# Two decoder blocks with product-key experts on one core: the search for experts spread over the blocks of weights, and three blocks multiplied in f32

## The chip, the cores and the metric

The kernel runs on 1 core of one Trainium2 chip, as one program. The metric is the device time of one execution in microseconds (us); the median of the runs counts.

## The reference, cut to what matters

256 tokens of width 1024 go through two decoder blocks. The first has four mixers (attention with forget gates, gated delta rule, two gated linear attentions) and a convolved gated FFN. The second has two attentions and, as its FFN, product-key retrieval over 16384 experts. All is f32. The part around the change is this FFN:

```python
q = (xc @ w_query).reshape(PEER_TOKEN_CHUNK, PEER_HEADS, 2, PEER_HALF)
s1 = jnp.einsum('thd,hnd->thn', q[:, :, 0], sub_keys_1)
s2 = jnp.einsum('thd,hnd->thn', q[:, :, 1], sub_keys_2)
v1, i1 = lax.top_k(s1, 16)
v2, i2 = lax.top_k(s2, 16)
cand = v1[..., :, None] + v2[..., None, :]
cand_idx = i1[..., :, None] * 128 + i2[..., None, :]
best, pos = lax.top_k(cand, 16)
idx = jnp.take_along_axis(cand_idx, pos, axis=-1)
g = jax.nn.softmax(best, axis=-1)
act = jax.nn.gelu(jnp.einsum('td,thkd->thk', xc, expert_u[idx]), approximate=False)
return jnp.einsum('thk,thkd->td', g * act, expert_v[idx])
```

(xc is the normed token, 8 heads, 16 experts a head.)

## The kernel before, in words

**Dense experts.** The kernel gathers experts only for 32 tokens (NG). For the other 224 (NT) it multiplies every expert: `expert_u` is walked in 64 blocks of 256 experts ("block q", the first pass), then `expert_v` in 64 blocks (the second pass). A block is 1 MB, a tile of 128 x 2048 f32. It is loaded by SP's queue into one of three slots of a ring of five (slots 0 to 2; a fourth, slot 3, joins in the second pass). Since TensorE (PE) multiplies f16 faster than f32, a block is split into two f16 halves that are scaled by 64: ACT writes the high half (`expert_hi`, line 2886), DVE the low half (`expert_lo`, line 2139), and PE makes three f16 products for one f32 product (`three`, lines 678, 681 and 684). So a block of the first pass is 2 x 8 x 3 = 48 matmuls of 128 x 224 (`expert_in`). The tokens are kept as f16 halves `xh`, `xl` as well.

**Buffers of halves.** There are seven. Numbers 0 to 3 take blocks 0 to 3; after that numbers 4, 5 and 6 rotate. They lie over `HT` (4, the f32 tokens), `X` (5) and ring slot 4 (6, in which the sub-keys land). `expert_hi(n)` waits until PE has finished block n-3. Six blocks (EARLY) are split before the search begins, while PE still makes the queries; the tables EARLY_HI and EARLY_LO say after which query group.

**The barrier.** After the queries all engines meet in `phase(1)` (DVE's side is line 1392). Then PE multiplies queries by sub-keys (line 1274, 32 f32 products), ACT copies them out of PSUM (line 2450), and DVE starts the search.

**The search on DVE.** `chosen` is a chain of 37 pieces: 12 of choosing for tokens 0 to 127 (`choose(0)`, lines 2154 to 2180), 6 of naming (`name_slots(0)`, lines 2192 to 2243), 8 of `choose(1)`, `slots_evicted(0)`, 4 more of `choose(1)`, 6 of `name_slots(1)`. The last piece of a naming waits for ACT's exponentials (line 2953, `gate_exp`). DVE runs 8 pieces first, and then one list per block q: `slots_evicted(1)` in the list behind the second SLOTS_AFTER; `one_hots` (lines 2275, 2278, 2280) for block q+1 if that has gates; `expert_lo(q+2)`; SEARCH[q] pieces of `chosen` (two for q = 0, 1, 2, then one); `weigh` of block q-1's gates (line 2289); `weigh_late(q-1)` (line 2303); and the gathered rows. An engine works its list strictly in order.

**ACT's list for block q:** `gelu(q)` (lines 2912, 2915; it waits for PE's block q), the exponentials if q is in EXP_AFTER, `expert_hi(q+3)`, `gated_hi` for block q+2 (line 2924), `keep_gates` of block q (line 2934).

**Gates.** `slots(t)` turns the named slots over on PE behind the blocks of SLOTS_AFTER (13 and 26); it waits for `slots_named`. From block LATE = 28 to block 61, 28 groups of 8 tokens are expanded to dense gates: one group is 16 matmuls of 128 columns (line 1314), woven into the block from its 13th matmul on. GATES_IN leaves out blocks 33, 38, 44, 49, 55 and 60. PE waits inside the block for `one_hots`.

**Loads.** SP's queue issues the loads in order. A load waits until its slot's last content has been read, which the list `read` in `sync_program` says: for a block of experts it is `expert_lo` of the block three before.

**Gathered rows.** For the 32 tokens POOL gathers 32 rows of `expert_u` and 32 of `expert_v` per partition (line 3203, 0.5 MB each) into three buffers `fetched`. The first three are issued as soon as the names are there; each further one waits for DVE (`row_in`, line 2316). DVE takes one in list 64 and from there five in four lists (the lists of the second pass are 64 to 127).

Of the kernel before, what the change touches and what calls it, by code (L numbers as in the profile page):

```python
# [34 lines left out]
GROUPS = NT // 8  # L35
EARLY = 6
LATE = 28
EARLY_LO = {3: (0,), 4: (1,), 5: (2, 3, 4), 7: (5,)}
EARLY_HI = {3: (0,), 4: (1, 2), 5: (3,), 6: (4, 5)}
SLOTS_AFTER = (13, 26)  # L40
EXP_AFTER = (8, 22)
GATES_IN = {LATE + (61 - LATE) * g // (GROUPS - 1): g for g in range(GROUPS)}
SEARCH = {**{q: 1 for q in range(64)}, 0: 2, 1: 2, 2: 2}
# [199 lines left out]
def memory(nc):  # L243
# [184 lines left out]
    m.halves_h, m.halves_l = ([f16(b_[:, 1024 * i:1024 * (i + 1)]) for b_ in first + [ht, x_, spare]] for i in range(2))  # L428
# [6 lines left out]
    m.fetched = [g.take(1024) for _ in range(3)]  # L435
# [217 lines left out]
def tensor_program(k):  # L653
# [623 lines left out]

    def expert_in(q):

        kk = k.halves(q)  # L1280
# [3 lines left out]
        pe.wait_ge(s["expert_lo"], q + 1)  # L1284
# [35 lines left out]
    for q in range(64):  # L1320
        expert_in(q)
        if q in SLOTS_AFTER:
            slots(SLOTS_AFTER.index(q))

    acc = [ps.take(pe, "acc", i, hold=True, counted=False) for i in range(4)]

    def expert_out(q, banks):

        kk = k.halves(64 + q)
# [10 lines left out]
    def expert_out_ready(q):  # L1340
        pe.wait_ge(s["expert_lo"], 64 + q + 1)
        pe.wait_ge(s["w_lo"], q + 1)
# [34 lines left out]
def vector_program(k):  # L1377
# [978 lines left out]
    for q in range(64):  # L2356
# [4 lines left out]
        if q + 2 >= EARLY:  # L2361
            expert_lo(q + 2)
# [15 lines left out]
    for q in range(64):  # L2378
        if q + 2 < 64:
            expert_lo(64 + q + 2)  # L2380
# [49 lines left out]
def scalar_program(k):  # L2430
# [440 lines left out]
    def expert_hi(n):  # L2871
# [4 lines left out]
        elif n == 4:  # L2876
            na.wait_ge(s["h_split"], 12)
        elif n == 5:
            na.wait_ge(s["x_kept"], 32)
        elif n == 6:  # L2880
            na.wait_ge(*ps.full("sub", 1, 3))
        elif 7 <= n < 67:
            na.wait_ge(*ps.full("u", n - 3))
        elif n >= 67:
            na.wait_ge(s["v_done"], n - 66)
# [17 lines left out]
    def gelu(q):  # L2903

        n = k.gated(q)
        src = ps.tile("u", q)[:, :].rearrange("p (j n) -> p j n", j=2)
        scale = UN
# [19 lines left out]
    def keep_gates(g):  # L2927

        n = 2 * k.answered(g)
        if g == 0:  # L2930
            na.wait_ge(s["rows_placed"], 16 * 3 * NK)
# [11 lines left out]
    for q in range(64):  # L2943
# [10 lines left out]
        if q == 0:  # L2954
            expert_hi(EARLY)
        if q + 3 > EARLY:
            expert_hi(q + 3)
# [6 lines left out]
    for q in range(64):  # L2964
        if q + 2 < 64:
            w_hi(q + 2)
        if q + 3 < 64:
            expert_hi(64 + q + 3)
# [35 lines left out]
def gpsimd_program(k):  # L3004
# [179 lines left out]
    ng.dma_start(m.fetched[2], k.d["ffn_g"]).then_inc(s["row_gain_landed"], 16)  # L3184
# [10 lines left out]
    for i in range(4):  # L3195
        at = slice(i * 256, (i + 1) * 256)
        ng.tensor_tensor(m.h_rows[:, at], m.h_rows[:, at], m.fetched[2][:, at], ALU.mult).then_inc(s["h_rows"], 1)
    for n in range(2 * NG):
        if n == 2:
            ng.wait_ge(s["h_rows"], 4)  # L3200
        if n >= 3:
# [9 lines left out]
def sync_program(k):  # L3211
# [10 lines left out]
    read += [(s["expert_lo"], n + 1) for n in range(128)]  # L3222
# [33 lines left out]
def program(nc, d, out):  # L3256
# [36 lines left out]
    def expert(n):  # L3293
        return k.ld.u[n] if n < 64 else k.ld.v[n - 64]
# [111 lines left out]
```

## Time and profile before

| | |
|---|---|
| median of 3 runs | 1283.02 us (1281.88 to 1285.21) |
| the profiled execution: time, span | 1282.18 us, 1280.9 us |
| PE busy | 1221.1 us (95%) |
| weight loads of PE | 1032.8 us (81%) |
| DVE busy | 1038.9 us (81%) |
| ACT busy | 681.3 us (53%) |
| POOL busy | 312.1 us (24%) |
| chain that ended last | PE 72%, DVE 15%, DMA 6%, ACT 4%, issue 3% |
| moved | 266.44 MB, mean 208 GB/s |

Of the span, about 630 us belong to all that comes before the sub-keys, and 650 us to the search and the two passes over the experts. The slices of the page give PE 9 tenths or more from 224 us on, with one slice of 8 (672 to 704 us). Times in timelines are counted from the span's start. "Busy" of PE is modelled, so the rhythm of the blocks is better read from the instructions that follow a block on ACT.

### The profile page before, as it was taken

What the parts mean: (1) busy time and instruction counts of PE and PEld (TensorE: products, weight loads), DVE (VectorE), ACT (ScalarE), POOL (GpSimd) and SP (SyncE); (2) the same over time, 40 slices, a digit from 0 to 9 for tenths busy, and PEclk for the clock granted to TensorE, in tenths of its full rate; (3) what the DMA queues carried; (4) which work ended last, traced back from release to release, by engine and by line L of the source; (5) the groups of instructions that cost most, each with busy time, mean ns of one, the idle gap of its engine ahead of it and who ended that gap; (6) DMA issues with size and microseconds to landing.
All of it is one profiled execution on the core that took longest, in us unless ns stands there. A gap on an engine that the chain in (4) does not pass through costs nothing.

```text
span 1280.9 us, 26856 instructions
## 1 busy us (share of the span) xinstructions
PE 1221.1 (95%) x11398; PEld 1032.8 (81%) x11398; DVE 1038.9 (81%) x1615; ACT 681.3 (53%) x972; POOL 312.1 (24%) x202
## 2 busy tenths in 40 slices
PE   6899888999999999999998999999999999999997
PEld 5545774888844546648897999999999999999996
DVE  5865883899956766677897999899998888989884
ACT  5663231757635435646524457677665554445553
POOL 0322221244500000000104600000003656555640
PEclk9999998999999999999998999999999999999999
DMA  7430003755656332457715766555558999999981
GB/s 314 185 125 3 2 2 135 292 199 198 216 214 248 107 107 91 145 184 262 232 35 199 257 253 205 198 199 194 196 198 301 341 349 355 363 341 386 342 314 34
DMA packets 51352, 266.44 MB, mean 208 GB/s; under 512 B 5136, under 2 KB 5408, under 8 KB 32544
## 3 DMA queue, kind: packets, MB, share of 16 engines
q1 hardware_dynamic: 40192, 226.76, 49.5%
q0 software_dynamic: 10160, 35.96, 7.4%
q10 hardware_dynamic: 880, 1.99, 0.4%
q8 instruction: 91, 1.49, 0.4%
q14 instruction: 29, 0.24, 0.1%
HBM read 262.04 MB, written 2.10 MB: 206 GB/s over the span
## 4 chain that ended last, share of the span: by engine, by line
PE 72%; DVE 15%; DMA 6%; ACT 4%; issue 3%; DVEq 0%; ACTq 0%; POOL 0%; POOLq 0%
PE bank L678 21%; PE bank L684 20%; PE bank L681 20%; DMA arena<-in_expert_rows,arena 6%; PE bank L1107 2%; PE bank L1314 2%; PE bank L758 1%; DVE arena L2316 1%; DVE ring L1773 1%; DVE ring L2139 1%; PE bank L825 1%; DVE X L2139 1%; PE bank L775 1%; PE bank L668 1%; DVE HT L1549 1%
## 5 line engine op out<-in xcount | busy, mean ns | idle before, releaser
L678 PE MATMUL bank<-arena 128*128 128x256 f16 (+3 forms) x720 | 216.2, 307 | 0.6 <-DVE arena L1443 0.4
L681 PE MATMUL bank<-arena 128*128 128x256 f16 (+3 forms) x720 | 216.1, 307 | 0.0
L684 PE MATMUL bank<-arena 128*128 128x256 f16 (+3 forms) x720 | 215.9, 306 | 0.0
L1443 DVE SCALAR_TENSOR_TENSOR arena<-ring,arena 128x2048 f16<-128x2048 f32 (+1 forms) x59 | 133.8, 2272 | 31.8 <-ACT arena L2489 31.8
L3203 POOL DMA_INDIRECT arena<-in_expert_rows,arena x32 | 74.2, 2318 | 285.2 <-DVE arena L2316 284.4
L2489 ACT ACTIVATE arena<-ring 128x2048 f16<-128x2048 f32 (+1 forms) x59 | 111.2, 1891 | 28.9 <-PE bank L684 28.9
L2941 ACT CAST arena<-arena 128x448 f16<-128x448 f32 x64 | 36.0, 565 | 138.5 <-PE bank L684 135.2
L2139 DVE SCALAR_TENSOR_TENSOR HT<-ring,HT 128x2048 f16<-128x2048 f32 x42 | 96.1, 2288 | 9.1 <-ACT HT L2886 8.9
L3203 POOL DMA_INDIRECT arena<-in_expert_v,arena x32 | 86.0, 2687 | 63.6 <-DVE arena L2334 54.1
L678 PEld LDWEIGHTS bank<-arena 128*128 128x128 f16 x720 | 70.5, 98 | 36.7 <-issue 2.0
L684 PEld LDWEIGHTS bank<-arena 128*128 128x128 f16 x720 | 70.5, 98 | 36.6 <-issue 0.6
L2139 DVE SCALAR_TENSOR_TENSOR ring<-ring 128x2048 f16<-128x2048 f32 x42 | 96.3, 2294 | 3.9 <-ACT ring L2886 3.9
L681 PEld LDWEIGHTS bank<-arena 128*128 128x128 f16 x720 | 70.6, 98 | 34.6 <-issue 0.9
L2139 DVE SCALAR_TENSOR_TENSOR X<-ring,X 128x2048 f16<-128x2048 f32 x41 | 93.7, 2285 | 4.0 <-ACT X L2886 4.0
L678 PE MATMUL bank<-cst,ring 128*128 128x224 f16 x336 | 87.9, 262 | 7.3 <-DVE ring L2139 7.3
L678 PE MATMUL bank<-arena,HT 128*128 128x224 f16 x352 | 91.2, 259 | 1.8 <-DVE small L2307 1.8
L3018 POOL TENSOR_TENSOR small<-small,cst 128x1 f32<-128x1 f32 (+3 forms) x16 | 18.9, 1180 | 299.7 <-DVE small L1397 299.7
L684 PE MATMUL bank<-arena,HT 128*128 128x224 f16 x352 | 91.2, 259 | 0.0
L681 PE MATMUL bank<-small,HT 128*128 128x224 f16 x352 | 91.2, 259 | 0.0
L678 PE MATMUL bank<-arena,ring 128*128 128x224 f16 x336 | 87.0, 259 | 2.4 <-DVE small L2307 2.4
L678 PE MATMUL bank<-arena,X 128*128 128x224 f16 x336 | 87.0, 259 | 1.0 <-DVE small L2307 1.0
L681 PE MATMUL bank<-cst,ring 128*128 128x224 f16 x336 | 87.9, 262 | 0.0
(385 smaller groups left out, 3786.5 us busy)
## 6 DMA issues: line engine op xcount, KB each, us to landing
ring<-in_expert_u SPq DMA_DIRECT2D x64, 1024.0 KB
ring<-in_expert_v SPq DMA_DIRECT2D x64, 1024.0 KB
ring<-in_w_in_n SPq DMA_DIRECT2D x24, 1024.0 KB, 4.7
ring<-in_w_up_t SPq DMA_DIRECT2D x22, 1024.0 KB, 5.2
ring<-in_w_down_n SPq DMA_DIRECT2D x11, 1024.0 KB, 4.7
ring<-in_w_out_n SPq DMA_DIRECT2D x8, 1024.0 KB, 4.7
ring<-in_w_query_t SPq DMA_DIRECT2D x8, 1024.0 KB, 4.8
ring<-in_w_in_t SPq DMA_DIRECT2D x3, 1024.0 KB
```

What stands on the lines that cost most here:

```text
L668: tr = pe.transpose(b[:, i * 128:(i + 1) * 128], m.xs[n][:, t, c * 128:(c + 1) * 128], ident)
L678: pe.matmul(out_, stat[0], mov[0], start=start, stop=False, skip_group_check=shared)
L681: pe.matmul(out_, stat[0], mov[1], start=False, stop=False, skip_group_check=shared)
L684: return pe.matmul(out_, stat[1], mov[0], start=False, stop=stop, skip_group_check=shared)
L1107: mm = pe.matmul(b[:, :], m.MT[:, 4 * half + c, t * 128:(t + 1) * 128], piece[:, c, :], start=(half == 0 and c == 0), stop=(half == 1 and ...
L1314: mm = pe.matmul(b[:, i * 128:(i + 1) * 128], oh[:, 2 * hf + i // 2, 0, :, i % 2], mov, start=(part == 0), stop=(part == 1))
L1443: nv.scalar_tensor_tensor(out=lo, in0=ld.slot(i), scalar=W_UP, in1=hi, op0=ALU.mult, op1=ALU.subtract).then_inc(s["split_lo"], 1)
L2139: nv.scalar_tensor_tensor(out=m.halves_l[kk], in0=ld.slot(i), scalar=W_UP, in1=m.halves_h[kk], op0=ALU.mult, op1=ALU.subtract).then_inc(s[ ...
L2489: na.activation(hi, ld.slot(i), ACT.Copy, scale=W_UP).then_inc(s["split_hi"], 1)
L2941: na.copy(m.Wh[n % 2][:, :, 0:NT], m.answers[:, 2 * n:2 * n + 2, :]).then_inc(s["w_hi"], 1)
L3018: ng.tensor_tensor(ap, ap, K(m, "half")[:, 0:n], ALU.pow).then_inc(s["rstd"], 1)
L3203: ng.indirect_dma_start(out=m.fetched[n % 3], out_offset=None, in_=k.d["expert_rows" if n < NG else "expert_v"], in_offset=bass.IndirectOf ...
```

## The change

The search takes one piece per list from the start (SEARCH is 1, and 0 for q = 3). The exponentials come after blocks 6 and 25 (before: 8 and 22), `slots` after blocks 11 and 29 (13 and 26), and the gates begin with block 31 (28); they leave out blocks 40, 50 and 60 now. Five blocks are split before the barrier; the sixth (block 5) is split in lists 0 of ACT and DVE. `HT` stays as it is to the end of the first pass: the halves rotate over buffer 2, `X` and ring slot 4, and over `HT`, `X` and slot 4 only in the second pass. Blocks 38, 46 and 54 (WHOLE) are not split at all: PE multiplies the f32 block in its ring slot by the f32 tokens in `HT`, 16 f32 matmuls of 128 x 224, and the slot is given back when PE has finished the block. Buffer 2 covers two of the three `fetched` buffers, so their order is turned round: one gather is issued early, the second waits for the last block of the first pass (63), and the third is behind it in POOL's queue. The wait for `rows_placed` moves from `keep_gates` to `gelu(31)`.

```diff
@@ -33,14 +33,16 @@
 NT = S - NG
 NK = 128 // NG
 GROUPS = NT // 8
+WHOLE = [38, 46, 54]
+SPLIT = [q for q in range(64) if q not in WHOLE]
 EARLY = 6
-LATE = 28
-EARLY_LO = {3: (0,), 4: (1,), 5: (2, 3, 4), 7: (5,)}
-EARLY_HI = {3: (0,), 4: (1, 2), 5: (3,), 6: (4, 5)}
-SLOTS_AFTER = (13, 26)
-EXP_AFTER = (8, 22)
+LATE = 31
+EARLY_LO = {3: (0,), 4: (1,), 5: (2, 3, 4)}
+EARLY_HI = {3: (0,), 4: (1, 2), 5: (3, 4)}
+SLOTS_AFTER = (11, 29)
+EXP_AFTER = (6, 25)
 GATES_IN = {LATE + (61 - LATE) * g // (GROUPS - 1): g for g in range(GROUPS)}
-SEARCH = {**{q: 1 for q in range(64)}, 0: 2, 1: 2, 2: 2}
+SEARCH = {**{q: 1 for q in range(64)}, 3: 0}
 
 
 
@@ -425,14 +427,14 @@
     x_ = m.X.rearrange("p t n -> p (t n)")
     ht = m.HT.rearrange("p c n -> p (c n)")
     first = [t[:, at:at + 2048] for at in (8704, 10752, 29696)] + [lent]
-    m.halves_h, m.halves_l = ([f16(b_[:, 1024 * i:1024 * (i + 1)]) for b_ in first + [ht, x_, spare]] for i in range(2))
+    m.halves_h, m.halves_l = ([f16(b_[:, 1024 * i:1024 * (i + 1)]) for b_ in first + [x_, spare, ht]] for i in range(2))
     a = Arena(t, 32768, END)
     m.oh_lo = [f16(a.take(512), 4, 128, 2) for _ in range(2)]
     m.oh = [f16(lent[:, 1024 * k:1024 * (k + 1)], 4, 2, 128, 2) for k in range(2)]
     g = Arena(t, 128 * NT, 32768)
     m.h_rows = g.take(1024)
     m.row_sums = m.h_rows
-    m.fetched = [g.take(1024) for _ in range(3)]
+    m.fetched = [g.take(1024) for _ in range(3)][::-1]
     g = Arena(t, 33792, END)
     m.row_at = g.take(NG).bitcast(U32)
     m.row_gate, m.row_dots, m.row_sel = (g.take(NG) for _ in range(3))
@@ -1275,13 +1277,28 @@
                                start=True, stop=True)
             mm.then_inc(ps.fill("sub", t, q4), 1)
 
+    def expert_in_whole(q):
+
+        w = ld.slot(ld.u[q]).rearrange("p (j c n) -> p j c n", j=2, c=8)
+        b = ps.take(pe, "u", q)
+        between = gates(GATES_IN[q]) if q in GATES_IN else iter(())
+        pe.wait_ge(*ld.landed(ld.u[q]))
+        for j in range(2):
+            for c in range(8):
+                mm = pe.matmul(b[:, j * 256:j * 256 + NT], w[:, j, c, :], HT[:, c, NG:256], start=(c == 0), stop=(c == 7))
+                if 8 * j + c >= 4:
+                    next(between, None)
+        mm.then_inc(ps.fill("u", q), 1)
+        for _ in between:
+            pass
+
     def expert_in(q):
 
-        kk = k.halves(q)
+        kk = k.halves(SPLIT.index(q))
         w_h, w_l = (x_[kk].rearrange("p (j c n) -> p j c n", j=2, c=8) for x_ in (m.halves_h, m.halves_l))
         b = ps.take(pe, "u", q)
         between = gates(GATES_IN[q]) if q in GATES_IN else iter(())
-        pe.wait_ge(s["expert_lo"], q + 1)
+        pe.wait_ge(s["expert_lo"], SPLIT.index(q) + 1)
         for j in range(2):
             for c in range(8):
                 mm = three(b[:, j * 256:j * 256 + NT], (w_h[:, j, c, :], w_l[:, j, c, :]),
@@ -1318,7 +1335,10 @@
                     yield
 
     for q in range(64):
-        expert_in(q)
+        if q in WHOLE:
+            expert_in_whole(q)
+        else:
+            expert_in(q)
         if q in SLOTS_AFTER:
             slots(SLOTS_AFTER.index(q))
 
@@ -1326,7 +1346,7 @@
 
     def expert_out(q, banks):
 
-        kk = k.halves(64 + q)
+        kk = k.halves(len(SPLIT) + q)
         w_h, w_l = (x_[kk].rearrange("p (j c n) -> p j c n", j=2, c=8) for x_ in (m.halves_h, m.halves_l))
         for i in banks:
             for j in range(2):
@@ -1338,7 +1358,7 @@
         return mm
 
     def expert_out_ready(q):
-        pe.wait_ge(s["expert_lo"], 64 + q + 1)
+        pe.wait_ge(s["expert_lo"], len(SPLIT) + q + 1)
         pe.wait_ge(s["w_lo"], q + 1)
 
     def kept_turned(i):
@@ -2358,8 +2378,10 @@
             next(slots_evicted(1))
         if q + 1 in GATES_IN:
             one_hots(GATES_IN[q + 1])
-        if q + 2 >= EARLY:
-            expert_lo(q + 2)
+        if q == 0:
+            expert_lo(EARLY - 1)
+        if q + 2 >= EARLY and q + 2 not in WHOLE:
+            expert_lo(SPLIT.index(q + 2) if q < 62 else len(SPLIT) + q - 62)
         for _ in range(SEARCH.get(q, 0)):
             next(chosen, None)
         if q - 1 in GATES_IN:
@@ -2377,7 +2399,7 @@
     nv.tensor_scalar(m.row_sel, m.row_sel, W_UP, None, ALU.mult).then_inc(s["row_sel"], 1)
     for q in range(64):
         if q + 2 < 64:
-            expert_lo(64 + q + 2)
+            expert_lo(len(SPLIT) + q + 2)
             w_lo(q + 2)
         rows_turn(64 + q)
 
@@ -2874,15 +2896,11 @@
         if n == 3:
             na.wait_ge(s["split_lo"], 65)
         elif n == 4:
-            na.wait_ge(s["h_split"], 12)
+            na.wait_ge(s["x_kept"], 32)
         elif n == 5:
-            na.wait_ge(s["x_kept"], 32)
-        elif n == 6:
             na.wait_ge(*ps.full("sub", 1, 3))
-        elif 7 <= n < 67:
-            na.wait_ge(*ps.full("u", n - 3))
-        elif n >= 67:
-            na.wait_ge(s["v_done"], n - 66)
+        elif n >= 6 and k.halves_free(n):
+            na.wait_ge(*k.halves_free(n))
         na.activation(m.halves_h[kk], ld.slot(i), ACT.Copy, scale=W_UP).then_inc(s["expert_hi"], 1)
 
     added_and_normed("out2", 3, 57)
@@ -2903,8 +2921,10 @@
     def gelu(q):
 
         n = k.gated(q)
+        if q == min(LATE, 14336 // (2 * NT)):
+            na.wait_ge(s["rows_placed"], 16 * 3 * NK)
         src = ps.tile("u", q)[:, :].rearrange("p (j n) -> p j n", j=2)
-        scale = UN
+        scale = 1.0 if q in WHOLE else UN
         na.wait_ge(*ps.full("u", q))
         if n:
             if q - LATE >= 2:
@@ -2927,8 +2947,6 @@
     def keep_gates(g):
 
         n = 2 * k.answered(g)
-        if g == 0:
-            na.wait_ge(s["rows_placed"], 16 * 3 * NK)
         for hf in range(2):
             na.wait_ge(*ps.full("G", g, hf))
             na.activation(m.answers[:, n:128, 8 * g + 4 * hf:8 * g + 4 * hf + 4],
@@ -2952,9 +2970,9 @@
                 na.wait_ge(s["gate_in"], t + 1)
                 na.activation(m.slot_gate[t], m.slot_gate[t], ACT.Exp).then_inc(s["gate_exp"], 1)
         if q == 0:
-            expert_hi(EARLY)
-        if q + 3 > EARLY:
-            expert_hi(q + 3)
+            expert_hi(EARLY - 1)
+        if q + 3 >= EARLY and q + 3 not in WHOLE:
+            expert_hi(SPLIT.index(q + 3) if q < 61 else len(SPLIT) + q - 61)
         if q + 2 in GATES_IN:
             gated_hi(GATES_IN[q + 2])
         if q in GATES_IN:
@@ -2965,7 +2983,7 @@
         if q + 2 < 64:
             w_hi(q + 2)
         if q + 3 < 64:
-            expert_hi(64 + q + 3)
+            expert_hi(len(SPLIT) + q + 3)
         if 64 + q == ROW_GELU:
             na.wait_ge(s["rows_used"], NG)
             na.activation(m.row_dots, m.row_dots, ACT.Gelu).then_inc(s["row_gelu"], 1)
@@ -3181,7 +3199,7 @@
 
     for i in range(NK):
         ng.dma_start(m.h_rows[i * NG:(i + 1) * NG, :], m.xs[3][0:NG, 0, :]).then_inc(s["rows_placed"], 16)
-    ng.dma_start(m.fetched[2], k.d["ffn_g"]).then_inc(s["row_gain_landed"], 16)
+    ng.dma_start(m.fetched[0], k.d["ffn_g"]).then_inc(s["row_gain_landed"], 16)
     choose(0)
     ng.wait_ge(s["slots_named"], 1)
     for i in range(NK):
@@ -3194,10 +3212,12 @@
     ng.wait_ge(s["row_gain_landed"], 16)
     for i in range(4):
         at = slice(i * 256, (i + 1) * 256)
-        ng.tensor_tensor(m.h_rows[:, at], m.h_rows[:, at], m.fetched[2][:, at], ALU.mult).then_inc(s["h_rows"], 1)
+        ng.tensor_tensor(m.h_rows[:, at], m.h_rows[:, at], m.fetched[0][:, at], ALU.mult).then_inc(s["h_rows"], 1)
     for n in range(2 * NG):
-        if n == 2:
+        if n == 0:
             ng.wait_ge(s["h_rows"], 4)
+        if n == 1:
+            ng.wait_ge(*ps.full("u", [q for i, q in enumerate(SPLIT) if k.halves(i) == 2][-1]))
         if n >= 3:
             ng.wait_ge(s["rows_used"], n - 2)
         ng.indirect_dma_start(
@@ -3219,7 +3239,8 @@
     read += [ps.full("out", g, 1) for g in range(2)]
     read += [(s["split_lo"], j + 1) for j in range(65)]
     read += [ps.full("sub", 1, 3)]
-    read += [(s["expert_lo"], n + 1) for n in range(128)]
+    read += [ps.full("u", q) if q in WHOLE else (s["expert_lo"], SPLIT.index(q) + 1) for q in range(64)]
+    read += [(s["expert_lo"], len(SPLIT) + q + 1) for q in range(64)]
     for i, src in enumerate(ld.src):
         if i == ld.at["w_in_n"]:
             sp.dma_start(m.cst[:, 576:NCONST], k.d["consts"][:, 576:NCONST]).then_inc(s["rest_landed"], 16)
@@ -3291,11 +3312,20 @@
         return (k.s["proj_half"], (j - 2) // 2 + 1) if j % 2 == 0 else k.ps.full("proj", (j - 2) // 2, 1)
 
     def expert(n):
-        return k.ld.u[n] if n < 64 else k.ld.v[n - 64]
+        return k.ld.u[SPLIT[n]] if n < len(SPLIT) else k.ld.v[n - len(SPLIT)]
 
     def halves(n):
 
-        return n if n < 4 else 4 + (n - 4) % 3
+        if n < 6:
+            return n
+        return ((2 if n < len(SPLIT) else 6), 4, 5)[(n - 6) % 3]
+
+    def halves_free(n):
+
+        if n >= len(SPLIT) + 3:
+            return k.s["v_done"], n - len(SPLIT) - 2
+        last = [q for i, q in enumerate(SPLIT[:n]) if halves(i) == halves(n)] if halves(n) < 6 else WHOLE
+        return k.ps.full("u", last[-1]) if last else None
 
     def answered(g):
 
@@ -3308,7 +3338,7 @@
     k.kept = nc.dram_tensor("x_kept", (2, 128, D), F32, kind="Internal").ap()
     k.split_load, k.split_buffer = split_load, split_buffer
     k.first_load, k.first_buffer, k.first_read = first_load, first_buffer, first_read
-    k.halves = halves
+    k.halves, k.halves_free = halves, halves_free
     k.expert, k.answered, k.gated = expert, answered, gated
     tensor_program(k)
     vector_program(k)
```

## Rows read from the trace of the kernel before

**Rows 1.** Busy time by stage (window, length, busy us of each engine, granted clock, DMA share, GB/s).

```profile
860.00:960.00 100.00, 100.00 (x1141) 100.00 (x1139) 96.41 (x109) 66.19 (x143) 0.00 (x0) 1.00 0.56 197
...
1000.00:1100.00 100.00, 95.88 (x996) 94.99 (x994) 86.56 (x93) 49.55 (x42) 61.27 (x26) 1.00 0.94 348
```

**Rows 2.** Waits of PE over the whole span (total us, times, longest).

```profile
PE bank L678 <- DVE ring L2139: 7.3, 2, 5.4
...
PE bank L1274 <- DVEq L1392: 3.0, 1, 3.0
```

**Rows 3.** Timeline of ACT, first instruction after blocks 6, 8, 9 (start, length).

```profile
672.03 0.55 ACT L2915 ACTIVATE arena<-bank 128x448 f32<-128x448 f32 x1 [4.27 <-PE bank L684]
...
681.23 0.54 ACT L2915 ACTIVATE arena<-bank 128x448 f32<-128x448 f32 x1 [2.26 <-PE bank L684]
...
693.54 0.55 ACT L2915 ACTIVATE arena<-bank 128x448 f32<-128x448 f32 x1 [7.05 <-PE bank L684]
```

**Rows 4.** Timeline of DVE in the same stretch.

```profile
649.68 0.45 DVE L2180 CAST arena<-arena 128x256 f32<-128x256 uint32 x1
...
663.67 1.22 DVE L2231 TENSOR_REDUCE arena<-arena 128x128 f32<-128x1024 f16 x1
...
664.80 2.28 DVE L2139 SCALAR_TENSOR_TENSOR ring<-ring 128x2048 f16<-128x2048 f32 x1
...
683.42 0.29 DVE L2239 TENSOR_REDUCE arena<-arena 128x8 f32<-128x128 f32 x1 [7.50 <-ACT arena L2953]
```

**Rows 5.** The barrier: chain of waits, timelines of PE and ACT, one window (clock 0.50).

```profile
626.43 2.26 DVEq L1392
...
628.74 9.04 PE L1274 MATMUL bank<-ring,arena 128*128 128x128 f32 x64 [3.03 <-DVEq L1392]
...
636.92 0.59 ACT L2450 COPY arena<-bank 128x512 f32<-128x512 f32 x1 [0.31 <-PE bank L1274]
...
637.81 0.59 ACT L2450 COPY arena<-bank 128x512 f32<-128x512 f32 x1 [0.31 <-PE bank L1274]
...
631.00:632.00 1.00, 1.00 (x6) 0.50 0.96 352
```

**Rows 6.** Gate stage: timelines of DVE and ACT, rhythm of one block.

```profile
847.70 1.22 DVE L2275 TENSOR_TENSOR ring<-cst,small 128x2048 f16<-128x2048 f16 x1
...
853.50 1.22 DVE L2275 TENSOR_TENSOR ring<-cst,small 128x2048 f16<-128x2048 f16 x1
...
935.02 1.22 DVE L2275 TENSOR_TENSOR ring<-cst,small 128x2048 f16<-128x2048 f16 x1
...
941.30 1.22 DVE L2275 TENSOR_TENSOR ring<-cst,small 128x2048 f16<-128x2048 f16 x1
...
846.81 0.32 ACT L2912 ACTIVATE cst<-bank 128x176 f32<-128x176 f32 x1 [1.17 <-PE bank L684]
...
852.32 0.33 ACT L2912 ACTIVATE small<-bank 128x192 f32<-128x192 f32 x1 [0.94 <-PE bank L684]
```

**Rows 7.** Chain of waits: f32 products of 512 columns, 20 of them (two records each).

```profile
208.85 17.17 PE bank L1107 x40
```

**Rows 8.** From a slot given back to the loaded block's first reader, DVE and ACT.

```profile
609.00 2.28 DVE L2139 SCALAR_TENSOR_TENSOR arena<-ring,arena 128x2048 f16<-128x2048 f32 x1
...
616.10 1.91 ACT L2886 ACTIVATE ring<-ring 128x2048 f16<-128x2048 f32 x1 [1.88 <-DMA ring<-in_expert_u]
...
673.21 1.91 ACT L2886 ACTIVATE ring<-ring 128x2048 f16<-128x2048 f32 x1 [0.64 <-DMA ring<-in_expert_u]
```

**Rows 9.** Second naming: ACT after block 22, DVE's last instruction of the naming.

```profile
753.67 0.55 ACT L2915 ACTIVATE arena<-bank 128x448 f32<-128x448 f32 x1 [2.26 <-PE bank L684]
...
769.08 0.29 DVE L2243 TENSOR_TENSOR arena<-arena 128x128 f32<-128x128 f32 x1
```

**Rows 10.** A gather's issue on POOL and its reader on DVE.

```profile
980.88 2.88 POOL L3203 DMA_INDIRECT arena<-in_expert_rows,arena x1 [1.67 <-DVE arena L2316]
...
990.84 1.22 DVE L2316 CUSTOM_DVE_ANT_0 arena<-arena 128x1024 f32<-128x1024 f32 x1 [1.03 <-DMA arena<-in_expert_rows,arena]
```

## The prediction

> **What bounds the kernel now.** I read the busy time by stage first: in the gate stage PE is busy for all of 100 us, at full clock, with DVE at 96; while rows are gathered PE is busy for 96 [rows 1]. So time is lost only where PE waits, and PE work that is added costs its full length. The waits of PE name the places: two on DVE's low halves, 7.3 us together, and 3.0 at the barrier [rows 2]. The instruction that follows each block on ACT dates the blocks: blocks 7 and 8 take 4.60 each (672.03 to 681.23) and block 9 takes 12.31; ahead of block 6's end ACT waits for 4.27 instead of the usual 2.26 [rows 3]. So block 6 loses 2.0 and block 9 7.7, the latter more than its wait, as the clock falls behind it. DVE's timeline gives the causes: the low half of block 6 starts only at 664.80, behind seven search pieces of 2.16 each (649.68 to 664.80), when PE wants to begin at 665.4 (672.03 less 4.60 and 2.0); and DVE stands for 7.50 us on the exponentials, which ACT makes behind block 8, while the low half of block 9 is queued behind that wait [rows 4].
>
> **The change, term by term**, against the profiled execution (1282.18 us, 0.84 under the median of 1283.02).
>
> *Barrier: -3.9.* DVE has finished its last query copy at 626.43, then makes the low half of block 5 (2.26) and only then releases PE at 628.74 [rows 5]. That half is gone from there, so PE starts near 626.5: 2.2 us. PE's idle time falls from 3.0 to under 1. After the 3.0 us the granted clock stood at 0.50, the lower level; after the 2 us ahead of block 6 block 7 still took 4.60 [rows 3]. So I expect no fall: the sub-key products then run at the pace of the last two copies, 0.89 for four products, 32 in 7.1 instead of about 8.9 (block 0 starts at 642.4 less 4.6, near 637.7). Together 3.9; with the clock still falling, 2.2. ACT splits blocks 3 and 4 behind query group 5, which ends before that last copy, so it holds nothing.
>
> *First blocks: -9.7.* DVE's lists are shorter by four pieces ahead of the low half of block 6. I walked them: block 0 starts at 633.7; the eight pieces end 2.8 earlier than the 649.68 of before, at 647; low half of block 5 to 649 (due 656.7); three pieces to 656; low half of block 6 to 658 (due 661.3); from there each list is 2.2 for a half and 2.2 for a piece, against 4.60, so blocks 7 and 8 are 3 to 4 us early. The exponentials, with two table loads, follow block 6; block 9's high half is ready at 670, its low half at 672, due 675. The naming ends in list 10, after `gate_exp`. Both stalls go. What is late next is nothing until block 29; bounds -9 and -9.7.
>
> *Three whole blocks: +4.6.* f32 products of 512 columns take 17.17/20 = 0.859, four passes of 0.215 [rows 7]; the sub-keys' 128 columns 0.89/16 = 0.056 a pass [rows 5]. A pass of 224 f16 columns is 4.60/48 = 0.096, so a whole block is 64 of these, 6.13 instead of 4.60, +1.53 each. Bounds 1.4 and 2.2 each. The halves they spare (1.9 of ACT, 2.2 of DVE) buy nothing while PE is the bound. The sub-keys' pace, 224 ns a product with its loads, speaks against that.
>
> *Second slots: +1.4.* Block 22 ends at 753.67 and the naming at 769.37, three lists later [rows 9]. Now the exponentials follow block 25, and the last piece stands in list 29, one list further: one more half (2.2) and one more piece (1.2 for one instruction, twice that at most; 1.9 taken [rows 4]) make 15.7 + 4.1 = 19.8. PE stands at the slots after 4 x 4.60 = 18.4. Bounds 0 and 2. The first slots are named some 3 us in time.
>
> *Slot of a whole block: +3.5.* This is the wait the change adds. Before, a slot was free about two blocks ahead of PE; now block 41 is loaded only when PE ends 38 (call it T), and ACT's list 38 holds its high half behind `gelu(38)`. The nearest row: slot given back at 611.3, reader starts at 616.10, 4.8 later; the other one, 667.1 to 673.21, gives 6.1 [rows 8, 4]. With 4.8: high half to T+6.7, low half to T+8.9, `weigh` and `weigh_late` (1.2), `one_hots` (2.35), ready at T+12.5. PE runs block 39 (5.51 with gates [rows 6]) and 40 (4.60, no gates) and asks 1.25 into block 41, at T+11.6 (a whole block signals 0.25 early, with four gate matmuls left). Stall 0.9. With it DVE has lost its lead, and its list is longer than PE's block: 5.80 near block 41, 6.28 near 58, against 5.51 [rows 6]. Each gate block until the next gap then costs the difference. Summed the same way: behind 38 0.9+0.25; behind 46 0.1+0.05 (48 has gates, so the price falls on 49); behind 54 0.4, then 0.75, 0.8 and 0.3 at 58, 59 and 61. That is 3.55. Bounds 0 (the lead is larger than I think) and 8 (6.1 each time: three times 1.3 more, and the second half of the gates late as well).
>
> *Gathers: +0.2.* The second and third now start when block 63 ends. Issue to reader takes 9.9 [rows 10]; their readers stand about 11.3 and 16 behind that point, so they are covered, but the stretch moves 1 MB more while DMA is nearly full (0.94 a little later [rows 1]). Bounds 0 and 2. The moved wait for `rows_placed` costs nothing: those copies are issued when the first naming ends, some twenty blocks earlier.
>
> Sum: -3.9 - 9.7 + 4.6 + 1.4 + 3.5 + 0.2 = -3.9, so 1278.3 for a profiled execution like this one and 1279.1 as a median.
>
> **Rivals.**
> *No queue behind whole blocks.* PE was never idle in the gate stage although DVE's list was already longer than its block [rows 1, 6], so the lead may be larger than I reckon. Against it stands ACT's order, in which everything of list 38 waits for the load. Without that term: 1275.6. Chance 0.25.
>
> *Slower: the three loads share the engines.* When block 38 ends, loads 41, 42 and 43 are all free to go, since 42 and 43 only stood behind 41 in SP's queue. If they advance together instead of one by one, block 41 lands when nearly 3 MB have moved: some 8 us instead of 4.8. At each of three places 3.2 more, and about 1.5 for the second half of gates: +11.1 on my sum, 1290.2. It ends above the time before once the landing takes about 6, and 0.3% above it at about 7.1. For it speaks the 6.1 [rows 8]; against it that one queue has so far delivered blocks in turn. By the Trainium skill (DMA: Bandwidth & Descriptors, Queues, Rings and Completion Order) each engine consumes one queue's descriptors in ring order, which would keep block 41 first and give the 1279.1. Chance 0.10.
>
> *The landing is 6.1 each time*, alone on the queue: +4.6, 1283.7. Chance 0.13.
>
> *The first stalls stay in part*, because DVE's pieces are only moved, or the clock falls at the barrier all the same: 2 to 5 us back, 1281 to 1284. Chance 0.10.
>
> The case summed above has 0.42, with 1277.0 to 1281.5 as its own range.
>
> **How the numbers follow.** A difference of 0.3% (3.85 us, about what a measurement of this kernel can tell from no change) is reached at 1279.2, so my sum lies on the edge: half of its 0.42 is faster, half no change. With the first rival faster has 0.47 (0.25 + 0.21, and a little of the rest); no change has 0.42 (0.21, the landing of 6.1, most of the stalls in part); slower 0.11. The range takes in the first rival and leaves out the slower one's end: 1274.8 to 1285.5.
>
> **What would show it.** Right: PE waits about 1 us at the barrier and the clock stays; blocks 1 to 10 follow at 4.60; PE waits near 1.4 at the second slots; f32 records in `expert_in_whole`, 6.1 a block; ACT's `expert_hi` idle 4 us on DMA behind 38, 46 and 54, and PE waits of under 1 us on `one_hots` after 41, 49, 57. Wrong: blocks behind the whole ones without a wait of PE (first rival), `expert_hi` waiting 7 us or more there (second), a block 6 or 9 over 5 us, a whole block far from 6.1, or rows of the second pass that wait for gathers 1 and 2.

## The result and the profile after

The changed kernel takes 1290.43 us (median of 7 runs, 1289.14 to 1293.48), the one before 1285.21 beside it (7 runs, 1281.88 to 1286.56). The ratio is 1.0048, with a 95% interval of 1.0036 to 1.0061: slower by about 6 us, where 1279.1 and "faster or the same" had been predicted. The profiled executions are 1291.37 us (span 1290.1) after and 1282.18 (span 1280.9) before.

ACT's first instruction behind a block dates it, as in [rows 3]. Of the kernel after:

```profile
639.33 0.55 ACT L2935 ACTIVATE arena<-bank 128x448 f32<-128x448 f32 x1 [2.71 <-PE bank L686]
...
672.22 0.55 ACT L2935 ACTIVATE arena<-bank 128x448 f32<-128x448 f32 x1
676.13 0.55 ACT L2935 ACTIVATE arena<-bank 128x448 f32<-128x448 f32 x1 [1.57 <-PE bank L686]
680.73 0.55 ACT L2935 ACTIVATE arena<-bank 128x448 f32<-128x448 f32 x1 [2.25 <-PE bank L686]
...
722.46 0.55 ACT L2935 ACTIVATE arena<-bank 128x448 f32<-128x448 f32 x1 [2.26 <-PE bank L686]
734.79 0.55 ACT L2935 ACTIVATE arena<-bank 128x448 f32<-128x448 f32 x1 [9.98 <-PE bank L686]
...
975.53 0.54 ACT L2932 ACTIVATE small<-bank 128x448 f32<-128x448 f32 x1 [1.34 <-PE bank L686]
```

The rows are blocks 0, 7, 8, 9, 18, 19 and 63. Block 9 ends 41.40 us behind block 0, which is 9 x 4.60: both stalls of [rows 3] are gone. (Block 7's row is late only because ACT was at the exponentials.) The lost time is in block 19: 12.33 us. From block 0 to block 63 it is 336.20 us. In the kernel before, the same two instructions are 325.68 apart:

```profile
642.41 0.54 ACT L2915 ACTIVATE arena<-bank 128x448 f32<-128x448 f32 x1 [2.71 <-PE bank L684]
...
968.09 0.54 ACT L2912 ACTIVATE small<-bank 128x448 f32<-128x448 f32 x1 [1.34 <-PE bank L684]
```

So this stretch grew by 10.5. Block 0 comes 3.1 earlier, and from block 63 to the end there are 314.6 us against 312.8.

PE's waits from 600 to 985 us, to be set beside [rows 2]:

```profile
PE bank L680 <- DVE small L2276: 6.1, 1, 6.1
PE bank L1331 <- DVE ring L2300: 3.1, 5, 1.0
PE bank L1314 <- DVE arena L2263: 1.5, 1, 1.5
PE bank L1276 <- DVEq L1412: 0.9, 1, 0.9
PE bank L680 <- DVE small L2327: 0.8, 1, 0.8
```

L1276 is the barrier, L1314 the second slots, L1331 the gates, L2327 `w_lo` at the start of the second pass. The first row is in no step of the prediction. L2276 is the last line of `slots_evicted`, and the matmul of `expert_in` that waits for it reads no slot. The timelines of PE, DVE and ACT there:

```profile
728.51 0.37 PE L680 MATMUL bank<-cst,X 128*128 128x224 f16 x1 [6.09 <-DVE small L2276]
...
724.84 2.29 DVE L2159 SCALAR_TENSOR_TENSOR arena<-ring,arena 128x2048 f16<-128x2048 f32 x1
...
728.18 0.28 DVE L2276 SCALAR_TENSOR_TENSOR small<-bank,small 128x128 f16<-128x128 f32 x1
...
722.90 1.90 ACT L2904 ACTIVATE arena<-ring 128x2048 f16<-128x2048 f32 x1
```

**What PE waits for is a PSUM bank.** The banks go round in a fixed order. `slots(0)` behind block 11 takes one, blocks 12 to 19 take the next eight turns, and the eighth of them, block 19, is given the bank of the slots again. (The Trainium skill, PSUM — Partial Sum Buffer, Specifications (TRN2), states eight banks a partition; with that the trace agrees, as the wait comes on the eighth taking.) DVE empties the bank at 728.18, in list 19: `slots_evicted(0)` is the 27th piece, 8 are done ahead of the lists, and one a list without list 3 puts the 19th of the rest into list 19. Before, three lists had two pieces and list 3 had one, which put it into list 15, while the bank was asked for by block 21. And in list 19 it stands behind `expert_lo(21)` (724.84), which needs `expert_hi(21)` (722.90), which ACT begins once PE has finished block 18. So PE can't have the bank until some 6 us after the end of block 18. The clock takes a second price: the windows of 727 to 730 and 730 to 734 us (columns as in [rows 1]) show

```profile
727.00:730.00 3.00, 1.49 (x9) 1.21 (x10) 1.42 (x5) 0.00 (x0) 3.00 (x6) 0.50 0.64 180
730.00:734.00 4.00, 4.00 (x36) 3.72 (x34) 0.00 (x0) 0.00 (x0) 1.31 (x2) 0.81 0.71 246
```

The granted clock is at 0.50, the lower level, after a wait of 6.1. Block 19 costs 12.33 - 4.60 = 7.7: 6.1 of wait as its row gives it, 0.2 that the row leaves out (e3 shows why), and 1.5 of slow clock: the first 16 matmuls start 0.186 apart (728.51 to 731.48) where 0.096 is the pace at full clock.

**The barrier.** PE's sub-key products, and a window inside them; before, they were one group of 9.04 at clock 0.50 [rows 5]:

```profile
627.31 7.38 PE L1276 MATMUL bank<-ring,arena 128*128 128x128 f32 x64 [0.88 <-DVEq L1412]
...
631.00:632.00 1.00, 1.00 (x12) 1.00 (x11) 1.00 (x9) 0.59 (x1) 0.00 (x0) 1.00 0.96 221
```

A wait of 0.88, full clock, 7.38 for the products. What this gives is best counted from PE's last query product, which starts at

```profile
625.43 0.27 PE L684 MATMUL bank<-cst,arena 128*128 128x256 f16 x1
```

in the kernel before and at

```profile
626.17 0.27 PE L686 MATMUL bank<-cst,arena 128*128 128x256 f16 x1
```

in the kernel after. From there to the end of block 0 it is 16.98 us before (to 642.41) and 13.16 after (to 639.33): 3.8 less.

**Whole blocks.** PE at the start of block 38 (two records are one f32 product), and ACT behind it:

```profile
825.73 0.26 PE L686 MATMUL bank<-cst,X 128*128 128x224 f16 x1
825.83 2.07 PE L1288 MATMUL bank<-HT,ring 128*128 128x224 f32 x10
827.74 0.22 PE L1331 MATMUL bank<-ring 128*128 128x128 f16 x1
827.79 0.59 PE L1288 MATMUL bank<-HT,ring 128*128 128x224 f32 x2
828.23 0.22 PE L1331 MATMUL bank<-arena,ring 128*128 128x128 f16 x1
828.28 0.59 PE L1288 MATMUL bank<-HT,ring 128*128 128x224 f32 x2
...
833.42 0.26 PE L680 MATMUL bank<-cst,ring 128*128 128x224 f16 x1
...
845.92 0.22 PE L1331 MATMUL bank<-ring 128*128 128x128 f16 x1 [0.98 <-DVE ring L2300]
...
833.33 0.28 ACT L2932 ACTIVATE cst<-bank 128x128 f32<-128x128 f32 x1 [3.25 <-PE bank L1288]
...
838.02 1.91 ACT L2904 ACTIVATE X<-ring 128x2048 f16<-128x2048 f32 x1 [4.09 <-DMA ring<-in_expert_u]
```

The first five products take 827.74 - 825.83 = 1.91, 0.382 each. As soon as gate matmuls are woven in, a pair of one f32 and one f16 matmul takes 0.49 (827.74 to 828.23 to 828.72), where 0.382 + 0.056 = 0.44 would be expected. The block lasts 833.42 - 825.83 = 7.59. Its slot is given back at 833.32, the high half of block 41 starts 4.7 later, and the one-hots are there 12.6 after it.

### The profile page after: what moved, and what is told of

Read it like the earlier page. It is cut to its first block, busy times and chain, and to the rows that moved or that the text cites. A ratio compares the mean times of both kernels' runs of the same rounds, so it can differ in the third digit from the quotient of the medians.

```text
span 1290.1 us, 26739 instructions
## 1 busy us (share of the span) xinstructions
PE 1227.3 (95%) x11350; PEld 1034.0 (80%) x11350; DVE 1031.8 (80%) x1609; ACT 674.6 (52%) x966; POOL 311.2 (24%) x202
## 4 chain that ended last, share of the span: by engine, by line
PE 67%; DVE 17%; DMA 6%; ACT 5%; issue 4%; ACTq 0%; POOL 0%; DVEq 0%; POOLq 0%
PE bank L680 19%; PE bank L686 18%; PE bank L683 18%; DMA arena<-in_expert_rows,arena 5%; PE bank L1109 2%; PE bank L1288 2%; PE bank L1331 1%; DVE arena L2336 1%; DVE ring L2159 1%; PE bank L760 1%; DVE X L2159 1%; DMA ring<-in_expert_u 1%; DVE ring L1793 1%; DVE arena L2159 1%; PE bank L827 1%
## 5 line engine op out<-in xcount | busy, mean ns | idle before, releaser
L680 PE MATMUL bank<-cst,arena 128*128 128x224 f16 (+2 forms) x528 | 129.1, 254 | 0.4 <-DVE arena L1463 0.4
L686 PE MATMUL bank<-cst,arena 128*128 128x224 f16 (+2 forms) x528 | 129.2, 254 | 0.0
L683 PE MATMUL bank<-cst,arena 128*128 128x224 f16 (+2 forms) x528 | 129.2, 254 | 0.0
L680 PE MATMUL bank<-arena,X 128*128 128x224 f16 x352 | 91.2, 259 | 1.6 <-DVE small L2327 1.6
L686 PE MATMUL bank<-arena,X 128*128 128x224 f16 x352 | 91.2, 259 | 0.0
L683 PE MATMUL bank<-small,X 128*128 128x224 f16 x352 | 91.2, 259 | 0.0
L680 PE MATMUL bank<-arena,HT 128*128 128x224 f16 x336 | 87.0, 259 | 3.2 <-DVE small L2327 3.2
```

The costliest lines, as they stand in the source:

```text
L680: pe.matmul(out_, stat[0], mov[0], start=start, stop=False, skip_group_check=shared)
L683: pe.matmul(out_, stat[0], mov[1], start=False, stop=False, skip_group_check=shared)
L686: return pe.matmul(out_, stat[1], mov[0], start=False, stop=stop, skip_group_check=shared)
```

## The experiments

One number is more exact here than the whole time. Kernels that are alike up to the search end block 0 anywhere from 638.39 to 640.96 us, and the rest behind block 63 spreads from 312.5 to 316.7. The stretch from block 0 to block 63 repeats far better, as the table shows: two kernels that lose the same time there by different waits (slots 13, bank emptied a list earlier) are 0.01 apart. Each is from one profiled execution. The ratio is of all runs against those of the kernel before that were taken beside them: median 1284.68 (21 runs) for e1 to e4, 1285.51 (17 runs) for e5 to e8.

| kernel | median, us (n) | ratio (95%) | end of block 0 | block 0 to 63 |
|---|---|---|---|---|
| before | 1285.21 (7) | 1 | 642.41 | 325.68 |
| after | 1290.43 (7) | 1.0048 (1.0036 to 1.0061) | 639.33 | 336.20 |
| e1: slots behind 13 | 1282.77 (11) | 0.9984 (0.9975 to 0.9993) | 639.00 | 328.56 |
| e2: e1, gates behind f32 | 1280.24 (5) | 0.9959 (0.9946 to 0.9973) | 640.00 | 325.73 |
| e3: e1, no whole block | 1273.64 (5) | 0.9917 (0.9904 to 0.9931) | 640.21 | 320.47 |
| e4: e1, whole in gaps | 1283.40 (11) | 0.9990 (0.9980 to 1.0000) | 638.39 | 327.97 |
| e5: emptied a list earlier | 1282.69 (11) | 0.9983 (0.9974 to 0.9992) | 640.20 | 328.55 |
| e6: e3, three early gathers | 1274.14 (6) | 0.9918 (0.9903 to 0.9933) | 639.35 | 320.48 |
| e7: e6, slots (13, 30) | 1275.30 (5) | 0.9921 (0.9906 to 0.9935) | 640.96 | 318.77 |
| e8: before, new search only | 1277.83 (6) | 0.9948 (0.9930 to 0.9966) | 644.19 | 320.49 |

### e1: the first slots two blocks later

```diff
-SLOTS_AFTER = (11, 29)
+SLOTS_AFTER = (13, 29)
```

> The changed kernel with the first slots behind block 13 again (as before), nothing else. Theory (a PSUM bank): in the changed kernel the slots turned over behind block 11 keep their bank until DVE's list 19, and block 19 of PE asks for the same bank of the ring of eight, so PE waits 6.1 us and loses 7.7 with the fallen clock. Behind block 13 the bank is asked for by block 21, two lists later, so the wait is gone: block 19 takes 4.60, and the whole run is 7.7 us shorter than the changed kernel, near 1282.7 as a median (ratio to before 0.998). Rival (DVE is simply late in list 19, whatever bank): the wait stays or moves to block 20 or 21, and the time stays at 1290.

Measured: 336.20 falls to 328.56, by 7.64, and the whole time by 7.7 (medians). PE's waits from 640 to 985 us:

```profile
PE bank L1331 <- DVE ring L2300: 3.2, 5, 1.1
PE bank L1314 <- DVE arena L2263: 1.5, 1, 1.5
PE bank L680 <- DVE small L2327: 0.8, 1, 0.8
```

The row of L2276 is gone and the others stand as they were. One number of the change, 11 for 13, cost all that block 19 lost.

### e2: gates behind the f32 products

On e1; the gate matmuls of a whole block come after its 16 products:

```diff
-                if 8 * j + c >= 4:
-                    next(between, None)
```

> As e1_slots13, and in the three whole blocks the 16 gate matmuls stand behind the 16 f32 products and are no longer woven between them. Theory: in the changed kernel an f32 product followed by one f16 gate matmul takes 0.49 us where 0.383 + 0.056 = 0.44 was reckoned, so each of the 12 pairs pays 0.05, 0.6 us a block. Behind the products the whole block takes 6.13 + 0.9 = 7.0 instead of 7.6, so 0 to 1.8 us less than e1_slots13 (less where DVE is the one that is waited for). The gates are asked for 4.3 us later in these blocks. Rival (the f32 product itself is 0.44 among gates, because its weight load is exposed): the block stays at 7.6.

Measured: 2.83 less than e1 in the stretch, 2.5 in the medians, more than the 0 to 1.8 expected. PE in block 38, and its waits at gates:

```profile
818.77 6.23 PE L1288 MATMUL bank<-HT,ring 128*128 128x224 f32 x32
824.84 0.22 PE L1329 MATMUL bank<-ring 128*128 128x128 f16 x1
...
825.71 0.22 PE L1329 MATMUL bank<-arena,ring 128*128 128x128 f16 x1
```

```profile
PE bank L1329 <- DVE ring L2298: 2.4, 4, 0.8
```

All 16 products take 824.84 - 818.77 = 6.07, 0.379 each, and the gate matmuls 0.058 each behind them. The next block starts at 825.77, so this one lasts 7.00 instead of 7.59. The 6.13 of the prediction is right to 1% for f32 alone; weaving costs 12 pairs x 0.05 = 0.6 a block, 1.8 in all. The expectation had left out the rest: the waits on one-hots fall by 0.8 in the rows (3.2 to 2.4), and by 1.06 when they are counted by starts as in e3. 3 x 0.59 + 1.06 is the whole 2.83. Why alternation costs 0.05 a pair is not shown.

### e3: no whole block

```diff
-WHOLE = [38, 46, 54]
+WHOLE = []
```

> As e1_slots13 with no whole block: all 64 are split, over the same three buffers (2, X, slot 4). Theory (each whole block costs more than it gives): PE has 3 x (7.6 - 5.5) = 6.3 us less to do; ACT no longer waits 4.1 us for a load three times; but DVE's list of 5.8 to 6.3 us is longer than the 5.5 of a gate block and only three blocks have no gates, so its lead of about 4 us is used up between blocks 50 and 60 and some 2 to 4 us of waits on the one-hots come at the end. In sum 4 to 8 us less than e1_slots13, 1275 to 1279. Rival (the whole blocks pay for themselves, as DVE would be the bound without them): equal to e1_slots13 or slower, with over 6 us of waits of PE on DVE between blocks 41 and 61.

Measured: 8.09 less than e1 in the stretch, 9.1 in the medians, a little more than the 4 to 8 expected (this kernel's profiled execution, 1278.81, is its longest; the excess is behind block 63). The three whole blocks are a plain loss. The wait on one-hots does not go with them:

```profile
PE bank L1331 <- DVE ring L2300: 1.9, 4, 0.6
PE bank L1314 <- DVE arena L2263: 1.5, 1, 1.5
PE bank L680 <- DVE small L2327: 0.8, 1, 0.8
```

This trace also shows what such a wait costs beyond its row. PE at one of them:

```profile
929.56 0.26 PE L680 MATMUL bank<-cst,X 128*128 128x224 f16 x1
930.39 0.22 PE L1331 MATMUL bank<-ring 128*128 128x128 f16 x1 [0.57 <-DVE ring L2300]
```

The starts are 0.83 apart, where 0.096 would follow without the wait. So 0.73 is lost and 0.57 is shown, as the row counts from the modelled end of the matmul before (0.26 long): 0.17 more for each wait. A wait shorter than that has no row at all. In the changed kernel PE does this at the first gate matmul of block 42:

```profile
851.33 0.26 PE L680 MATMUL bank<-cst,ring 128*128 128x224 f16 x1
851.66 0.22 PE L1331 MATMUL bank<-ring 128*128 128x128 f16 x1
```

That is 0.23 lost; block 52 loses 0.14 and block 61 0.23 in the same way. Counted by starts, the waits at the gates are 4.5 us in the changed kernel, 4.6 in e1 and 2.8 in e3. So 1.8 of e1's belong to the whole blocks. With 3 x (7.59 - 5.51) = 6.2 of PE's own time (5.51 is a split block with gates, [rows 6]) this makes 8.1, all that e3 gains.

The remaining 2.8 are also in e8, which has the old buffers and no whole block, and not in the kernel before, so they come with the new search settings. The likely cause is that DVE's list is longer than PE's block, with three gaps between the gates instead of six; no run changes the gaps alone.

### e4: whole blocks where no gates are

```diff
-WHOLE = [38, 46, 54]
+WHOLE = [40, 50, 60]
```

> As e1_slots13 with the whole blocks moved to 40, 50 and 60, the ones without gates. Theory: no pairs of f32 and f16 products, so a whole block takes 6.1 and the three together 1.8 us less PE time than in e1_slots13; the load of block 43, 53, 63 still starts only when PE ends the whole block, and DVE still loses its lead there, now with gate blocks directly behind (41, 42, 43 in place of one gap): the stalls on the one-hots stay at 2 to 5 us. Together -3 to +1 against e1_slots13. Rival (the stalls come from where the whole blocks stand relative to the gaps, not from the load): no waits on the one-hots.

Measured: 327.97, only 0.6 under e1; medians 0.6 above it. The 1.8 for weaving is saved; the waits at the gates, counted by starts, grow from 4.6 to 5.8. The gaps, in which DVE could catch up, are now the whole blocks, and behind each of them a load is waited for. PE's waits, and ACT's on the loads:

```profile
PE bank L1331 <- DVE ring L2300: 3.9, 10, 0.6
PE bank L680 <- DVE small L2327: 2.0, 1, 2.0
```

```profile
ACT arena L2904 <- DMA ring<-in_expert_u: 12.7, 3, 4.2
```

ACT stands 4.2 at each of the three loads wherever they lie; more and shorter waits follow at the gates, and 2.0 at the start of the second pass (0.8 in e1), which lies behind the stretch.

### e5: the bank emptied one list earlier

The slots stay behind block 11; the pieces are one list earlier.

```diff
-SEARCH = {**{q: 1 for q in range(64)}, 3: 0}
+SEARCH = {**{q: 1 for q in range(64)}, 3: 1}
```

> The changed kernel with SEARCH[3] = 1 in place of 0, nothing else: every later piece of the search is one list earlier, so DVE empties the bank of the first slots in list 18 and not in 19; the slots stay behind block 11. Theory (block 19 of PE waits for that bank): the emptying ends about 6 us behind block 17, which is 1.4 behind block 18, so the wait shrinks from 6.1 to 1 to 2 us, the clock stays, block 19 takes about 6.2, the naming of the second slots is one list earlier too and their 1.5 us wait goes. Median near 1283 (1282 to 1285). Rival (what counts is only behind which block the slots stand): the wait stays at 6 and the time at 1290.

Measured: the wait is still there, and short.

```profile
724.78 0.27 PE L680 MATMUL bank<-cst,X 128*128 128x224 f16 x1 [1.49 <-DVE small L2276]
```

One list earlier is 4.60 earlier, and 6.09 - 4.60 = 1.49: exact. e1 moved the block that asks for the bank by two, which is more than the wait, and the wait went; this kernel moved the list that empties it by one, and the wait fell by just that. Block 19 takes 6.26 here (723.33 to 729.59), so the clock had no part in it. The stretch is 328.55, as e1's, since the wait at the second slots (1.5) is gone in exchange: the second naming ends a list earlier too.

### e6: halves and gathers as before

On e3, `HT` is in the rotation again and three gathers go early.

```diff
+        elif n == 6:
+            na.wait_ge(s["h_split"], 12)
...
-        if n == 1:
-            ng.wait_ge(*ps.full("u", [q for i, q in enumerate(SPLIT) if k.halves(i) == 2][-1]))
...
-        return ((2 if n < len(SPLIT) else 6), 4, 5)[(n - 6) % 3]
+        return (6, 4, 5)[(n - 6) % 3]
...
```

> As e3_none_whole, with the halves rotating over HT, X and slot 4 from block 6 on, as in the kernel before; buffer 2 is free after block 2, so all three first gathers are issued early and none waits for block 63. Still five blocks ahead of the barrier and the search of the changed kernel. Theory (the two late gathers cost something): the waits of PE behind L2307/L2327 in the second pass fall from 5.9 in e3_none_whole's profile to the 4.1 to 5.2 of the kernel before: 1 to 2 us less. Rival (those gathers are covered, the spread is noise): within 0.5 us of e3_none_whole.

Measured: 320.48 against 320.47 in the stretch, and e6's median is 0.5 above e3's, so the gain of 1 to 2 us did not come. The two late gathers are covered: in the changed kernel their readers start on DVE at 986.82 and 991.42, 11.3 and 15.9 us behind block 63, without a wait. Whether they slow the loads beside them isn't settled. PE's waits on `w_lo` from 985 to 1110 us are 4.8 here against 5.9 in e3, and over all kernels 3.6 to 4.8 in the four with early gathers and 4.5 to 5.9 in the six with late ones. That is 1 us on average, about what these runs scatter by.

### e7: the second slots one block later as well

```diff
-SLOTS_AFTER = (11, 29)
+SLOTS_AFTER = (13, 30)
```

(on e6's other edits)

> As e6_three_gathers with the second slots behind block 30 (29). They are asked for only from the 13th group of gates on. Theory: the 1.5 us wait of PE for the second naming goes, as block 30 ends 4.6 later; nothing else moves: 1.5 us less than e6_three_gathers. Rival (DVE, which is the longer list from there, is what PE meets anyway): the waits on the one-hots grow by as much and the time is the same.

Measured: the wait at L1314 is gone, and the stretch is 1.71 shorter than e6's (318.77). PE's waits from 640 to 985 us are only

```profile
PE bank L1331 <- DVE ring L2300: 1.9, 4, 0.6
PE bank L680 <- DVE small L2327: 0.8, 1, 0.8
```

The whole time does not show it (1275.30 against 1274.14, ranges that overlap): here block 0 ended 1.6 later, which is the spread of what lies ahead of it. A gain of 1.7 is below what these runs can tell.

### e8: the search alone, in the kernel before

```diff
-LATE = 28
-SLOTS_AFTER = (13, 26)
-EXP_AFTER = (8, 22)
+LATE = 31
+SLOTS_AFTER = (13, 29)
+EXP_AFTER = (6, 25)
...
-SEARCH = {**{q: 1 for q in range(64)}, 0: 2, 1: 2, 2: 2}
+SEARCH = {**{q: 1 for q in range(64)}, 3: 0}
```

> The kernel before with the search part of the change alone: one piece a list (none in list 3), exponentials behind blocks 6 and 25, slots behind 13 and 29, gates from block 31. Six blocks ahead of the barrier, the old buffers, three early gathers, no whole block. Theory: the two first stalls go (-9.7), the second slots cost 1.5, the gates that start later cost the 1.9 us of waits on one-hots that e3_none_whole shows: 6 us less than before, near 1278.5. Rival (the stalls are bound to the sixth block's halves and the barrier, not to the search): the stall of 2.0 or 7.7 stays.

Measured: 320.49, as e3 and e6 to 0.02. The barrier's wait is as before:

```profile
PE bank L1274 <- DVEq L1392: 3.0, 1, 3.0
PE bank L1314 <- DVE ring L2280: 1.9, 4, 0.6
PE bank L1297 <- DVE arena L2243: 1.5, 1, 1.5
PE bank L678 <- DVE small L2307: 0.8, 1, 0.8
```

So the search is worth -5.2 by itself (325.68 to 320.49). The sixth block's halves are the other gain. e6 and e8 differ in them, and otherwise only in how the buffers are numbered and in where ACT waits for `rows_placed`. From PE's last query product to the end of block 0 it is 16.98 us in e8, as in the kernel before, and 13.16 to 13.17 in the eight kernels with the move. The medians of e6 and e8 are 3.7 apart.

## Why the prediction was wrong, by its steps

The forecast was -3.9; the profiled executions differ by +9.2 and the runs by about +6.2 (the ratio on 1285.2). The terms, as predicted and as measured (waits counted by starts, as in e3):

| step | predicted | measured | from |
|---|---|---|---|
| barrier | -3.9 | -3.8 | 16.98 to 13.16; the clock stayed at 1.00 |
| first blocks | -9.7 | -9.7 | blocks 1 to 18 at 4.60 |
| bank of the first slots | none | +7.7 | e1, e5 |
| three whole blocks, f32 | +4.6 | +4.5 | 7.00 in e2 against 5.51 |
| f32 and f16 woven | none | +1.8 | 7.59 against 7.00, e2 |
| second slots | +1.4 | +1.7 | L1314 |
| waits on one-hots | +3.5 | +4.5 | L1331; 1.8 of it by the whole blocks |
| gathers | +0.2 | not settled | covered; 0 to about 1, e6 |

These measured terms make +6.7, against the +6.2 of the runs (interval 4.6 to 7.8). Without the barrier they make 10.5, which is what the stretch grew by. The 2.5 us between this and the +9.2 of the profiled executions lie outside: 0.7 ahead of the last query product, which is scatter, and 1.8 behind block 63, of which no run shows how much belongs to the change.

**The step that failed** is the sentence "What is late next is nothing until block 29", which rests on the one further on, "The first slots are named some 3 us in time". The second is true: the naming ends at 686.88, block 11 at 689.93. But the walk of the lists stopped at the naming. It asked when PE may take its bank for the slots, and not when PE would want that bank back. The 26 pieces ahead of `slots_evicted(0)` had been counted neither against the eight turns of the banks nor against a list that can't get to its end until some 6 us after the block before. PE waited 6.1 us for that bank in block 19 and lost 7.7. With that one row the sum would have been +3.8 instead of -3.9, inside "no change" and near its edge.

*The woven products* were a term that the prediction had at nothing, in a place where the nearest rows were all of one type of matmul. Together a whole block costs 7.59 - 5.51 = 2.08 more than a split one with gates [rows 6], near the upper of the bounds 1.4 and 2.2.
*The queue behind a whole block* came out as reckoned: slot given back at T = 833.32, PE asks at 844.94 (T+11.6, predicted T+11.6), one-hots there at 845.92 (T+12.6, predicted T+12.5), wait 0.98 by its row (predicted 0.9), 1.14 by starts. The waits at 57, 58, 59 and 61 (0.78, 0.73, 0.77 and 0.23) lie where 0.4, 0.75, 0.8 and 0.3 had been reckoned. But the term was near right for a reason partly wrong: 2.8 of the 4.5 are there with no whole block at all (e3, e8). The prediction had charged all of it to the whole blocks.

*The rivals.* No queue behind whole blocks: refuted, ACT waits 4.1 for the load at each (838.02, 884.66, 930.60) and PE up to 1.0 for the one-hots. Three loads sharing the engines: refuted in its mechanism, since those three waits of ACT are alike and the first ends 4.7 behind the slot given back, with two more loads released at the same time; the slower result came by another road. Landing of 6.1: refuted by the same rows. First stalls in part: refuted.

Was the whole idea sound? The search's new rhythm (-5.2) and the moved sixth block (-3.8) are gains; the three whole blocks lose 8.1 and buy nothing, since they spare ACT and DVE work where PE is the bound. Without them and with the slots behind 13 the kernel takes 1273.64 to 1275.30 (e3, e6, e7), 0.8% less than before.

## What to carry to other kernels

When work is moved within lists that run in step, follow each buffer to its second taking: count the takings of a rotating PSUM bank between the use that moves and the one that gets the same bank, and name the instruction that empties it and its place in its engine's list. A wait for a bank shows in the trace as a matmul that waits for an instruction whose output it never reads. Sparing an engine that isn't the bound pays only where it shortens a wait of the bound, and a block that skips the staging also gives its slot back last, so price the next load with it.

## What the runs showed of the hardware, unexpectedly

- An f32 matmul of 224 columns and an f16 one of 128 in turn take 0.49 us a pair, against 0.382 and 0.056 to 0.058 in runs of one type; 0.6 a block.
- After a wait of PE of 6.1 us the granted clock was at 0.50, and the slow matmuls cost another 1.5. Waits of 0.9 to 1.5 (barrier, L1314, e5) cost their own length and 0.2. In the kernel before, the clock was at 0.50 behind a wait of 3.0 [rows 5], and the block behind a loss of 2.0 still took 4.60 [rows 3].
- A wait of PE read from a row leaves out 0.17 us, and one of less than that has no row: three such, 0.14 to 0.23 by starts, made 0.6 us in the changed kernel. Counted by starts the terms of the stretch add up to what it grew by, within 0.1 us; by rows 1.6 would be missing.
- From PE's last query product to the end of block 0 it took 13.16 to 13.17 us in eight kernels, while the end of block 0 itself moved by 2.6; the 63 blocks behind it repeated to 0.02. Compare a stretch between two fixed instructions before comparing whole times.
